# First projection in two half-depth steps between the modulation loads, and the first gates after the second chunk

## The chip, the cores and the metric

The kernel runs on one core of a Trainium2 chip. The time is the device time of one execution in microseconds; of several executions the median counts. Five queues work side by side: TensorE (PE), VectorE (DVE), ScalarE (ACT), GpSimd (POOL) and SyncE (SP), which here issues most of the loads.

## The reference

One layer of a diffusion backbone on 128 context tokens and 256 sample tokens (T = 384 columns), with 1024 channels. What matters for this case is its beginning:

```python
mod = silu(cond) @ w_ada + b_ada            # w_ada: 1024 x 6144
sh1, sc1, g1, sh2, sc2, g2 = split(mod, 6)
h = rmsnorm(x, g_norm1) * (1 + sc1) + sh1
u = h @ w_in                                # w_in: 1024 x 7168
b_c, c_c, v_c, x_r, g_r, m_a, m_b = split(u)
y_a = (b_c * conv3(c_c * v_c)) @ w_conv_out
x_c = conv4(x_r) + rnn_conv_b
# two linear scans over x_c, with gates sigmoid(x_c @ w_gate + b): 8 heads of 128
# then y_b, the merged branches @ w_o, and a mixture of 32 experts of width 512
```

sh1 and sc1 are the first 2048 columns of the modulation: four chunks of 512 columns.

## The kernel before

**Chunks and tiles.** Weights come in chunks of 1024 x 512 (2,048 KB) into a ring of four slots; `chunks` is the order of the loads. SyncE issues chunk n as soon as the one four places before it has been used (L546 to L566). Each chunk gives four output tiles of 128 channels x 384 tokens, m = 0 to 3. `stream` is the order of all tiles, and tile n lies in PSUM bank n % 8, so that a tile can only begin when the tile eight places before it has been read (`open_tile`, `bank_free`). `START` and `W_IN` are the two lists of the work at the beginning: ("par", j) transposes parameters, ("xT", k) transposes a slice of 128 channels of the normalised x, ("adaR", j) multiplies the conditioning with modulation chunk j into rows, ("adaC", j) turns these rows into columns; then come the chunks of `w_in`: ("xr", half), ("c", half), ("v", half) and so on, and a bare number b stands for the gates of two heads, batch b.

**Split products.** The projections multiply in a faster 32-bit form, with both operands split into a high and a low part. A tile takes three products for each slice k of the depth: high weights by low x and by high x (the high parts, L889 and L890; L869 and L870 in the first projection), and low weights by high x (L893; L874). The weights are split by quarters of a chunk, q: ScalarE writes the high part (`feed`, L1262), GpSimd subtracts it for the low part (`write_lo`, L478). There are three pairs of buffers (SUBS = 3). VectorE scales and shifts x (L1699), ScalarE takes its high part (L1316), VectorE its low part (L1692); `h_ready` counts the slices done.

**The first projection** (`first_project`) takes three tiles of ("xr", 0) together, slice by slice, over the whole depth of eight slices, when all four modulation chunks are in; VectorE itself writes the low parts of these three quarters. The fourth tile follows in the usual way. Ahead of it stand products of constants, without use (`constants`, L911).

**Behind the first chunk.** ScalarE copies tile ("xr", h) into one of two padded buffers (`copy_xr`, L1327 and L1328) and, behind the copy, splits the quarter that is three further on (`feed_behind`). From the third copy on it waits for the convolution two tiles before it (`xc_ready`). VectorE convolves (`conv_rnn`: one instruction at L1712, three at L1716), and computes the decay rates once (L1728 to L1742). TensorE's gates for a head (L903) need that head's convolution; ScalarE's sigmoids read them (L1340), and its exponents (L1356, L1361) and a root (L1366) follow, with VectorE between (`gate_inputs`) and behind (`scans`, from L1761). `conv_grid` reads the tiles of ("v", half) from L1792 on. The order on each engine is the order in which the code is written.

Of the kernel before, what the change touches and what calls it, by code (L numbers as in the profile page):

```python
# [40 lines left out]
def layer_program(nc, x_prompt, x_sample, state_rnn, c, c_ctx, w_ada, b_ada, g_norm1, g_norm2, w_in,  # L41
# [71 lines left out]
    def add_gates(b):  # L113
        for h in (2 * b, 2 * b + 1):
            for d in range(2):
# [11 lines left out]
    START = [("par", 0), ("par", 1), ("adaR", 0), ("xT", 0), ("xT", 1), ("xT", 2), ("xT", 3), ("adaR", 1),  # L127
             ("adaC", 0), ("xT", 4), ("xT", 5), ("xT", 6), ("xT", 7), ("adaR", 2), ("adaC", 1),
             ("adaC", 2), ("adaR", 3), ("adaC", 3)]
    stream += START  # L130
    chunks += [("ada", j) for j in range(4)]
    ADA_AFTER = {("v", 0): 4, ("b", 0): 5, ("g", 0): 6, ("c", 1): 7, ("v", 1): 8, ("b", 1): 9, ("g", 1): 10,
                 ("ma", 0): 11}
    for item in W_IN:
        if isinstance(item, int):
            add_gates(item)
        else:
            add_chunk(*item)
# [24 lines left out]
    with ExitStack() as ctx:  # L163
# [160 lines left out]
        first_lo = sem("first_lo_by_vector")  # L324
# [130 lines left out]

        def wait_sub_free(eng, q):

            if q >= SUBS:
                wait_quarter_used(eng, q - SUBS)
# [6 lines left out]
        def wait_split(eng, q):  # L466

            if q < SUBS:
                eng.wait_ge(first_lo, q + 1)
            else:  # L470
                eng.wait_ge(lo_p, q - SUBS + 1)

        def write_lo(eng, q, done):

            src, pair = quarter(q)
            eng.wait_ge(hi_ready, q + 1)
            for ks in (slice(0, KD // 2), slice(KD // 2, KD)):
                last = eng.tensor_tensor(pair[:, 1, ks], src[:, ks], pair[:, 0, ks].bitcast(F32), ALU.subtract)  # L478
            last.then_inc(done, 1)
# [4 lines left out]
        def wait_chunk_used(eng, n):  # L484
# [3 lines left out]
            elif n < NSPLIT:  # L488
                if SPLIT.index(n) == 0:
                    wait_split(eng, SUBS - 1)  # L490
# [169 lines left out]
        def _(eng):  # L660
# [30 lines left out]
            for q in range(SUBS, NQ):  # L691
                write_lo(eng, q, lo_p)
# [103 lines left out]
        def _(eng):  # L796
# [63 lines left out]
            def first_project(kind, x):  # L860

                tiles = [open_tile((kind, m)) for m in range(SUBS)]
                pairs = [quarter(quarter_of(kind, m))[1] for m in range(SUBS)]
                for k in range(KD):
                    eng.wait_ge(h_ready, k + 1)
                    for m in range(SUBS):
                        if k == 0:
                            eng.wait_ge(hi_ready, m + 1)
                        eng.matmul(tiles[m][:, 0:T], pairs[m][:, 0, k, :], x[:, 1, k, :], start=(k == 0), stop=False)  # L869
                        eng.matmul(tiles[m][:, 0:T], pairs[m][:, 0, k, :], x[:, 0, k, :], start=False, stop=False)  # L870
                for m in range(SUBS):
                    wait_split(eng, m)
                    for k in range(KD):
                        mm = eng.matmul(tiles[m][:, 0:T], pairs[m][:, 1, k, :], x[:, 0, k, :],  # L874
                                        start=False, stop=(k == KD - 1))
                    mm.then_inc(tile_done, 1)
                project(kind, 0, x, range(SUBS, CT))

            def project(kind, half, x, ms=range(CT), ready=None):

                for m in ms:
# [3 lines left out]
                    eng.wait_ge(hi_ready, q + 1)  # L885
# [27 lines left out]
            spare = N_OF[("adaR", 2)] % BANKS  # L913
            assert spare == N_OF[("xr", SUBS)] % BANKS
            for name, number in START:
                if (name, number) == ("adaC", 3):
                    constants(spare, 1)
                start_work[name](number)
                if (name, number) == ("adaC", 2):
                    constants(spare, 1)  # L920
            constants(spare, 4)
            for n, item in enumerate(W_IN):
# [4 lines left out]
                else:  # L927
                    if n == 0:
                        first_project(item[0], h_hl)
# [308 lines left out]
        def _(eng):  # L1238
# [13 lines left out]
            fed = [0]  # L1252
# [48 lines left out]
            eng.wait_ge(mean_ready, 1)  # L1301
            eng.activation(stat[:, 0, 2, :], stat[:, 0, 1, :], ACT.Sqrt).then_inc(rms_ready, 1)
# [5 lines left out]
            for name, number in START[2:]:  # L1308
                if name == "xT":
                    ps, free = tile(("xT", number))  # L1310
                    eng.activation(xTr[:, number, :], ps[:, 0:T], ACT.Copy).then_inc(free, 1)
                elif name == "adaR":
                    ada_copy(number)
            for k in range(KD):
                eng.wait_ge(h_whole, k + 1)
                eng.activation(h_hl[:, 0, k, :], xTr[:, k, :], ACT.Copy).then_inc(act_hi, 1)  # L1316
                if 1 <= k <= SUBS:
                    feed(k - 1)
# [49 lines left out]
            def copy_c(half):  # L1368
                for m in range(CT):
# [244 lines left out]
        def _(eng):  # L1614
# [27 lines left out]

            eng.wait_ge(ssq_ready, TT)
# [3 lines left out]
            for t in range(TT):  # L1647
                eng.tensor_scalar(xs[:, t, :], x_in_rows[:, t, :], stat[:, 0, 0, t:t + 1], None, ALU.mult)\
                    .then_inc(xs_ready, 1)
                if t == 1:  # L1650
                    copy_params()
# [29 lines left out]
            for j in range(4):  # L1681
                ada_columns(j)
            for j in range(4):
                wait_read(eng, ("adaC", j))
            for cnd in range(2):
                last = eng.scalar_tensor_tensor(out=A1[:, :, cnd], in0=mod[:, KD:2 * KD, cnd], scalar=1.0,
                                                in1=pT[:, GN1:GN1 + KD], op0=ALU.add, op1=ALU.mult)
# [585 lines left out]
```

## Time and profile before

| | us |
|---|---|
| median of three executions | 949.86 |
| lowest, highest | 949.2, 952.07 |
| the profiled execution | 951.76 |
| its span | 949.7 |

| engine | busy share of the span |
|---|---|
| TensorE | 93% |
| VectorE | 60% |
| GpSimd | 35% |
| ScalarE | 30% |

The busy shares are means over a projection stage of some 390 us, a short stage of routing, and 32 experts. A busy TensorE counts from the start of a matmul to its modelled end, so that two matmuls which follow each other overlap; the distance from start to start is what a matmul costs in a row. The granted clock is given as a share of 2.4 GHz; 0.5 is 1.2 GHz. Times on the left of the rows are microseconds from the start of the span.

### The profile page before, as it was taken

What the parts mean: (1) busy time and instruction counts of PE and PEld (TensorE: products, weight loads), DVE (VectorE), ACT (ScalarE), POOL (GpSimd) and SP (SyncE); (2) the same over time, 40 slices, a digit from 0 to 9 for tenths busy, and PEclk for the clock granted to TensorE, in tenths of its full rate; (3) what the DMA queues carried; (4) which work ended last, traced back from release to release, by engine and by line L of the source; (5) the groups of instructions that cost most, each with busy time, mean ns of one, the idle gap of its engine ahead of it and who ended that gap; (6) DMA issues with size and microseconds to landing.
All of it is one profiled execution on the core that took longest, in us unless ns stands there. A gap on an engine that the chain in (4) does not pass through costs nothing.

```text
span 949.7 us, 12700 instructions
## 1 busy us (share of the span) xinstructions
PE 885.1 (93%) x4502; PEld 551.9 (58%) x4502; DVE 571.0 (60%) x990; ACT 282.9 (30%) x499; POOL 333.4 (35%) x301
## 2 busy tenths in 40 slices
PE   3899999999999999999999999998988988989895
PEld 1579988989999999755444344333333333433331
DVE  2489984677102342236477777775766666766677
ACT  4366374645334332021321121121212121211112
POOL 0046946556556646122222232231313131313100
PEclk9999999999999999999999999999999999999998
DMA  9962556464572537637699999999999999999992
GB/s 344 356 256 89 184 178 220 162 240 172 183 263 91 187 120 250 240 158 291 240 393 411 410 411 419 414 416 402 409 394 415 396 403 389 406 404 408 402 419 87
DMA packets 61882, 285.70 MB, mean 301 GB/s; under 512 B 6895, under 2 KB 11279, under 8 KB 47492
## 3 DMA queue, kind: packets, MB, share of 16 engines
q1 hardware_dynamic: 58228, 278.63, 75.9%
q0 software_dynamic: 2480, 3.11, 1.1%
q10 hardware_dynamic: 1120, 3.24, 0.9%
q8 instruction: 34, 0.56, 0.2%
q14 instruction: 20, 0.16, 0.0%
HBM read 286.80 MB, written 3.19 MB: 305 GB/s over the span
## 4 chain that ended last, share of the span: by engine, by line
PE 65%; DMA 26%; DVE 3%; SPq 2%; ACT 2%; issue 1%; DVEq 0%; ACTq 0%; POOL 0%
DMA ring<-in_w 13%; DMA slot<-in_w 11%; PE bank L889 10%; PE bank L890 10%; PE bank L893 10%; PE bank L1113 9%; PE bank L1130 7%; PE bank L959 4%; PE bank L1114 3%; DMA ring<-in_w_ada 2%; PE bank L1090 2%; PE bank L825 2%; PE bank L903 2%; PE bank L1068 1%; SPq L637 1%
## 5 line engine op out<-in xcount | busy, mean ns | idle before, releaser
L478 POOL TENSOR_TENSOR subs<-ring,subs 128x512 fp32r<-128x512 f32 x138 | 205.5, 1514 | 176.5 <-ACT subs L1262 176.5
L889 PE MATMUL bank<-h_hl,subs 128*128 128x384 f32 x488 | 165.9, 340 | 0.6 <-ACT lru L1340 0.6
L890 PE MATMUL bank<-h_hl,subs 128*128 128x384 f32 x488 | 164.1, 336 | 0.0
L1113 PE MATMUL bank<-ring,x_T 128*64 128x512 f32 x256 | 116.7, 597 | 11.7 <-DMA slot<-in_w 4.3
L1114 PE MATMUL bank<-ring,x_T 128*64 128x512 f32 x256 | 117.1, 598 | 0.0
L2079 DVE TENSOR_TENSOR hg<-hg,lru 128x512 f32<-128x512 f32 x186 | 116.7, 680 | 0.0
L676 POOL COPY idx<-lists 64x1 uint32 (+1 forms) x31 | 5.5, 179 | 297.3 <-PE bank L1068 292.8
L1113 PE MATMUL bank<-slot,x_T 128*64 128x512 f32 x192 | 89.2, 606 | 11.5 <-DMA slot<-in_w 8.2
L1262 ACT ACTIVATE subs<-ring 128x1024 fp32r<-128x1024 f32 x72 | 76.1, 1060 | 72.6 <-PE bank L893 72.6
L889 PEld LDWEIGHTS bank<-h_hl,subs 128*128 128x128 f32 x488 | 91.7, 188 | 5.8 <-issue 4.2
L893 PE MATMUL bank<-h_hl,subs 128*128 128x384 f32 x488 | 94.7, 336 | 0.0
L1554 ACT ACTIVATE lru<-bank 64x512 f32<-64x512 f32 x32 | 19.0, 595 | 247.8 <-PE bank L1114 247.8
L890 PEld LDWEIGHTS bank<-h_hl,subs 128*128 128x128 f32 x488 | 91.7, 188 | 0.4
L1114 PE MATMUL bank<-slot,x_T 128*64 128x512 f32 x192 | 89.6, 607 | 0.0
L893 PEld LDWEIGHTS bank<-h_hl,subs 128*128 128x128 f32 x488 | 85.6, 188 | 0.0
L2070 DVE TENSOR_TENSOR lru<-bank,gain_sample 128x512 f32<-128x512 f32 x124 | 78.9, 674 | 0.0
L2097 DVE SCALAR_TENSOR_TENSOR xcy<-bank,weight_col,lru 64x256 f32<-64x256 f32 x64 | 37.3, 662 | 65.0 <-ACT lru L1554 64.6
L1113 PEld LDWEIGHTS bank<-ring,x_T 128*64 128x64 f32 x256 | 32.7, 136 | 72.5 <-issue 67.2
L2070 DVE TENSOR_TENSOR lru<-bank,cp 128x512 f32<-128x512 f32 x62 | 40.0, 686 | 57.8 <-PE bank L1090 57.8
L689 POOL COPY weight_col<-slot_weight 64x1 f32 (+1 forms) x32 | 69.9, 2187 | 3.2 <-DVE slot_weight L2126 3.2
L1547 ACT ACTIVATE y_hl<-bank 64x512 fp32r<-64x512 f32 x62 | 36.7, 592 | 103.8 <-PE bank L1132 103.1
L1090 PE MATMUL bank<-y_hl,token_oh 128*128 128x512 f32 x186 | 59.4, 427 | 0.0
(249 smaller groups left out, 1504.2 us busy)
## 6 DMA issues: line engine op xcount, KB each, us to landing
ring<-in_w SPq DMA_DIRECT2D x40, 2048.0 KB, 29.2
slot<-in_w SPq DMA_DIRECT2D x30, 2048.0 KB, 29.0
ring<-in_w_in SPq DMA_DIRECT2D x14, 2048.0 KB, 8.0
ring<-in_w_ada SPq DMA_DIRECT2D x12, 2048.0 KB, 8.9
gate_w<-in_w SPq DMA_DIRECT2D x10, 2048.0 KB, 30.0
ring<-in_w SPq DMA_DIRECT2D x16, 1024.0 KB, 31.0
slot<-in_w SPq DMA_DIRECT2D x12, 1024.0 KB, 31.7
ring<-in_w_rnn_out SPq DMA_DIRECT2D x2, 2048.0 KB, 8.3
```

Of the source, the lines that this page charges most:

```text
L478: last = eng.tensor_tensor(pair[:, 1, ks], src[:, ks], pair[:, 0, ks].bitcast(F32), ALU.subtract)
L689: eng.tensor_copy(weight_col[:, s:s + 1], slot_weight[:, bass.ds(e, 1)]).then_inc(weight_cols, 1)
L889: eng.matmul(ps[:, 0:T], pair[:, 0, k, :], x[:, 1, k, :], start=(k == 0), stop=False)
L890: eng.matmul(ps[:, 0:T], pair[:, 0, k, :], x[:, 0, k, :], start=False, stop=False)
L893: mm = eng.matmul(ps[:, 0:T], pair[:, 1, k, :], x[:, 0, k, :], start=False, stop=(k == KD - 1))
L1090: eng.matmul(bank[SPREAD[b % 3]][:, :], token_oh[s % 2][:, t * P:(t + 1) * P], y_hl[:, half, :], start=True, stop=True).then_inc(spread_do ...
L1113: eng.matmul(ps[HALF:P, :], x_T[:, k, :], w1_k[:, k, :], start=(k == 0), stop=(k == KD - 1))
L1114: mm = eng.matmul(ps[0:HALF, :], x_T[:, k, :], w3_k[:, k, :], start=(k == 0), stop=(k == KD - 1))
L1130: eng.matmul(ps[0:HALF, :], zT_buf[:, j * HALF:(j + 1) * HALF], w[:, j, 0:CW], start=(j == 0), stop=(j == JF - 1))
L1262: eng.activation(pair[:, 0], src, ACT.Copy).then_inc(hi_ready, 1)
L2070: eng.tensor_tensor(y_gated[:, b % 3, :], bank[SPREAD[b % 3]][:, :], G2[0 if t == 0 else 1][:, half * CW:(half + 1) * CW], ALU.mult).then_ ...
L2079: eng.tensor_tensor(rows, rows, y_gated[:, b % 3, :], ALU.add).then_inc(added, 1)
```

## The change

The order of the loads becomes modulation 0, modulation 2, ("xr", 0), modulation 1, modulation 3, ("xr", 1): modulation chunks 0 and 2 hold shift and scale of the first four slices of x, chunks 1 and 3 those of the last four. The first projection takes all four tiles of ("xr", 0), first over slices 0 to 3, then over slices 4 to 7, with the products of modulation chunks 1 and 3 between the matmuls of the first half. The weights of ("xr", 0) are split in eight half-quarters r; the last two reuse the buffer of the first two, and `half_used` tells that those are free. GpSimd writes all low parts, and waits for `h_ready` of 4 before the first. VectorE does the scale, the shift and the split of x in two halves. Gates 0 come behind ("xr", 1) instead of ahead of it, on TensorE, ScalarE and VectorE. Silu goes ahead of the root, VectorE's copies of the parameters go first, and of the constants two are left.

```diff
-    W_IN = [("xr", 0), 0, ("xr", 1), ("c", 0), ("v", 0), 1, ("b", 0), ("g", 0), 2, ("c", 1), ("v", 1), 3,
+    W_IN = [("xr", 0), ("xr", 1), 0, ("c", 0), ("v", 0), 1, ("b", 0), ("g", 0), 2, ("c", 1), ("v", 1), 3,
...
+    START = [("par", 0), ("par", 1), ("adaR", 0)] + [("xT", k) for k in range(KD)] + \
+        [("adaR", 2), ("adaC", 0), ("adaC", 2)]
+    stream += START + [("adaR", 1), ("adaC", 1), ("adaR", 3), ("adaC", 3)]
+    chunks += [("ada", 0), ("ada", 2), ("xr", 0), ("ada", 1), ("ada", 3)]
...
+        def half_quarter(r):
+
+            m, k0 = r % CT, (KD // 2) * (r // CT)
+            part = r % (2 * SUBS)
+            cols = slice((part % 2) * (QUART // 2), (part % 2 + 1) * (QUART // 2))
+            return slot_k(C_OF[("xr", 0)])[:, k0:k0 + KD // 2, m * P:(m + 1) * P], \
+                subs[:, part // 2, :, cols].rearrange("p x (k n) -> p x k n", k=KD // 2)
+
         def wait_sub_free(eng, q):
 
-            if q >= SUBS:
+            if q == CT:
+                eng.wait_ge(half_used, 1)
+            else:
                 wait_quarter_used(eng, q - SUBS)
...
-            for q in range(SUBS, NQ):
-                write_lo(eng, q, lo_p)
+            eng.wait_ge(h_ready, CT)
+            for r in range(2 * CT):
+                write_half_lo(eng, r)
+            for q in range(CT, NQ):
+                write_lo(eng, q)
...
+            def first_project(x):
+
+                K2 = KD // 2
+
+                def high_parts(k):
+
                     eng.wait_ge(h_ready, k + 1)
-                    for m in range(SUBS):
+                    for m in range(CT):
+                        r = CT * (k // K2) + m
                         if k == 0:
...
+                        if k % K2 == 0:
+                            eng.wait_ge(hi_ready, r + 1)
+                        ps, pair = bank[N_OF[("xr", m)] % BANKS], half_quarter(r)[1]
+                        eng.matmul(ps[:, 0:T], pair[:, 0, k % K2, :], x[:, 1, k, :], start=(k == 0), stop=False)
+                        eng.matmul(ps[:, 0:T], pair[:, 0, k % K2, :], x[:, 0, k, :], start=False, stop=False)
+
+                def low_parts(r):
+
+                    ps, pair = bank[N_OF[("xr", r % CT)] % BANKS], half_quarter(r)[1]
+                    eng.wait_ge(lo_p, r + 1)
+                    for j in range(K2):
+                        k = K2 * (r // CT) + j
+                        mm = eng.matmul(ps[:, 0:T], pair[:, 1, j, :], x[:, 0, k, :], start=False, stop=(k == KD - 1))
+                    return mm
+
+                for k in range(K2):
+                    if k == K2 - 1:
+                        ada_rows(1)
+                    high_parts(k)
+                low_parts(0)
+                ada_columns(1)
+                low_parts(1)
+                ada_rows(3)
+                low_parts(2)
+                low_parts(3).then_inc(half_used, 1)
+                ada_columns(3)
+                for k in range(K2, KD):
+                    high_parts(k)
+                for m in range(CT):
+                    low_parts(CT + m).then_inc(tile_done, 1)
...
             for name, number in START:
-                if (name, number) == ("adaC", 3):
-                    constants(spare, 1)
                 start_work[name](number)
-                if (name, number) == ("adaC", 2):
-                    constants(spare, 1)
-            constants(spare, 4)
+                if (name, number) == ("adaR", 0):
+                    constants(spare, 2)
...
+            half_hi(4)
+            ada_copy(1)
+            half_hi(5)
+            ada_copy(3)
+            half_hi(6)
+            half_hi(7)
+            h_hi(4)
+            h_hi(5)
+            feed(CT)
+            h_hi(6)
+            h_hi(7)
...
-            copy_xr(2)
-            copy_xr(3)
+            for h in range(2, KD):
+                copy_xr(h)
             gate_sigmoids(0)
             gate_exps(0)
-            copy_xr(4)
-            copy_xr(5)
+            copy_c(0, range(0, 3))
             gate_roots(0)
-            copy_xr(6)
-            copy_xr(7)
-            copy_c(0)
+            copy_c(0, range(3, CT))
...
+            for half in range(2):
+                ks = range(CT * half, CT * (half + 1))
+                for j in (half, 2 + half):
+                    ada_columns(j)
+                for j in (half, 2 + half):
+                    wait_read(eng, ("adaC", j))
...
-            for q in range(SUBS):
-                write_lo(eng, q, first_lo)
...
             decay_rates()
-            conv_rnn(2)
-            conv_rnn(3)
+            for h in range(2, KD):
+                conv_rnn(h)
             gate_inputs(0)
-            for h in range(4, KD):
-                conv_rnn(h)
             scans(0)
```

TensorE before, from the first modulation rows to the first projection (ring and cvec: modulation rows; ident and lru: transposes of x; selc and xcy: modulation columns; iota and ones: constants):

```order
L825 MATMUL bank<-ring,cvec 32x512 x8
L814 MATMUL bank<-ident,lru 128x128 x12
L825 MATMUL bank<-ring,cvec 32x512 x8
L835 MATMUL bank<-selc,xcy 128x2 x4
L814 MATMUL bank<-ident,lru 128x128 x12
L825 MATMUL bank<-ring,cvec 32x512 x8
L835 MATMUL bank<-selc,xcy 128x2 x8
L911 MATMUL bank<-iota,ones 128x384
L825 MATMUL bank<-ring,cvec 32x512 x8
L911 MATMUL bank<-iota,ones 128x384
L835 MATMUL bank<-selc,xcy 128x2 x4
L911 MATMUL bank<-iota,ones 128x384 x4
```

TensorE now, from the first modulation rows to the end of the first half of the sums (L890 the high parts, of which the repeats are left out, L899 the low parts):

```order
L841 MATMUL bank<-ring,cvec 32x512 x8
L950 MATMUL bank<-iota,ones 128x384 x2
L830 MATMUL bank<-ident,lru 128x128 x24
L841 MATMUL bank<-ring,cvec 32x512 x8
L851 MATMUL bank<-selc,xcy 128x2 x8
...
L841 MATMUL bank<-ring,cvec 32x512 x8
...
L899 MATMUL bank<-h_hl,subs 128x384 x4
L851 MATMUL bank<-selc,xcy 128x2 x4
L899 MATMUL bank<-h_hl,subs 128x384 x4
L841 MATMUL bank<-ring,cvec 32x512 x8
L899 MATMUL bank<-h_hl,subs 128x384 x8
L851 MATMUL bank<-selc,xcy 128x2 x4
```

Two of the four modulation products moved behind the first matmuls of the projection; the columns product of chunk 3 is now the last thing ahead of its second half, and the four constants that stood ahead of the projection are gone.

ScalarE before, around the first sigmoids (xrp: copy of an ("xr", h) tile, subs: high part of a quarter, lru<-bank: sigmoids):

```order
L1327 ACTIVATE xrp<-bank 128x128
L1328 ACTIVATE xrp<-bank 128x256
L1262 ACTIVATE subs<-ring 128x1024
L1340 ACT_TABLE_LOAD
L1340 ACTIVATE lru<-bank,pT 128x387 x8
L1356 ACT_TABLE_LOAD
L1356 ACTIVATE lru<-lru,rate 128x387 x4
L1361 ACTIVATE lru<-lru,rate 128x387 x4
L1327 ACTIVATE xrp<-bank 128x128
```

ScalarE now, at the same sigmoids (cp: copy of a ("c", m) tile):

```order
L1393 ACTIVATE xrp<-bank 128x128
L1394 ACTIVATE xrp<-bank 128x256
L1297 ACTIVATE subs<-ring 128x1024
L1406 ACT_TABLE_LOAD
L1406 ACTIVATE lru<-bank,pT 128x387 x8
L1422 ACT_TABLE_LOAD
L1422 ACTIVATE lru<-lru,rate 128x387 x4
L1427 ACTIVATE lru<-lru,rate 128x387 x4
L1439 ACTIVATE cp<-bank 128x128
```

Before, the copies ahead of the sigmoids were those of tiles 0 to 3 and the other four followed; now all eight stand ahead, each with a quarter's high part from the third on, and the tiles of ("c", 0) follow.

## Rows read from the trace of the kernel before

**Rows 1.** The page: busy time, share of the span and instructions of each engine.

```profile
PE 885.1 (93%) x4502; PEld 551.9 (58%) x4502; DVE 571.0 (60%) x990; ACT 282.9 (30%) x499; POOL 333.4 (35%) x301
```

**Rows 2.** Waits of TensorE, 66 to 560 us: total, times, longest.

```profile
PE bank L968 <- DVE hg L1917: 1.2, 1, 1.2
...
```

**Rows 3.** Chain of waits, 0 to 150 us: start, us, what.

```profile
10.47 19.72 DMA ring<-in_w_ada
```

**Rows 4.** Timeline of TensorE: start, us to last end, instructions, idle before and releaser.

```profile
16.02 3.64 PE L825 MATMUL bank<-ring,cvec 128*32 128x512 f32 x16 [6.30 <-ACT cvec L1306]
19.59 1.63 PE L814 MATMUL bank<-ident,lru 128*128 128x128 f32 x12
...
25.36 1.92 PE L825 MATMUL bank<-ring,cvec 128*32 128x512 f32 x16
27.21 1.95 PE L835 MATMUL bank<-selc,xcy 128*128 128x2 f32 x16
29.02 0.89 PE L911 MATMUL bank<-iota,ones 128*128 128x384 f32 x2
30.33 3.47 PE L825 MATMUL bank<-ring,cvec 128*32 128x512 f32 x16 [0.42 <-DMA ring<-in_w_ada]
...
35.49 2.83 PE L911 MATMUL bank<-iota,ones 128*128 128x384 f32 x8
...
49.60 4.32 PE L874 MATMUL bank<-h_hl,subs 128*128 128x384 f32 x24
...
57.93 2.76 PE L903 MATMUL bank<-xcy,gate_w 128*128 128x387 f32 x8
62.20 2.87 PE L903 MATMUL bank<-xcy,gate_w 128*128 128x387 f32 x8 [1.51 <-DVE xcy L1716]
...
82.43 0.34 PE L889 MATMUL bank<-h_hl,subs 128*128 128x384 f32 x1
...
117.66 5.47 PE L903 MATMUL bank<-xcy,gate_w 128*128 128x387 f32 x16
```

**Rows 5.** Stretches: length, busy PE, PEld, DVE, ACT, POOL, granted clock, DMA share, GB/s.

```profile
30.00:32.00 2.00, 1.67 (x8) 0.46 (x12) 0.00 (x0) 0.00 (x0) 0.00 (x0) 0.52 1.05 385
32.00:34.00 2.00, 2.00 (x13) 0.50 (x6) 0.00 (x0) 0.14 (x1) 0.00 (x0) 0.63 1.06 390
...
60.00:62.00 2.00, 0.69 (x3) 0.07 (x1) 1.96 (x2) 0.00 (x0) 1.72 (x2) 1.00 1.05 398
```

**Rows 6.** Timeline of VectorE.

```profile
37.65 0.56 DVE L1692 TENSOR_TENSOR h_hl<-hg,h_hl 128x384 fp32r<-128x384 f32 x1
...
57.53 4.61 DVE L1716 SCALAR_TENSOR_TENSOR xcy<-xrp,pT,xcy 128x387 f32<-128x387 f32 x3
62.06 0.16 DVE L1728 TENSOR_SCALAR sp<-sp 128x16 f32<-128x16 f32 x1
...
67.42 0.48 DVE L1712 TENSOR_SCALAR xcy<-xrp,pT 128x387 f32<-128x387 f32 x1
67.93 1.94 DVE L1716 SCALAR_TENSOR_TENSOR xcy<-xrp,pT,xcy 128x387 f32<-128x387 f32 x3
...
98.94 2.86 DVE L1761 TENSOR_TENSOR lru<-lru 128x1548 f32<-128x1548 f32 x1
...
120.41 0.41 DVE L1793 TENSOR_TENSOR cp<-bank,cp 128x256 f32<-128x256 f32 x1
```

**Rows 7.** Timeline of GpSimd: low parts beside the first convolutions.

```profile
52.83 8.89 POOL L478 TENSOR_TENSOR subs<-ring,subs 128x512 fp32r<-128x512 f32 x6 [50.38 <-ACT subs L1262]
```

**Rows 8.** Timeline of ScalarE: a copy, a quarter's high part, the first sigmoids.

```profile
62.24 0.28 ACT L1327 ACTIVATE xrp<-bank 128x128 f32<-128x128 f32 x1 [4.33 <-DVE xcy L1716]
...
62.67 1.06 ACT L1262 ACTIVATE subs<-ring 128x1024 fp32r<-128x1024 f32 x1
63.75 1.28 ACT L1340 ACT_TABLE_LOAD   x1
65.05 3.91 ACT L1340 ACTIVATE lru<-bank,pT 128x387 f32<-128x387 f32 x8
```

More of the change, by code:

```diff
@@ L137, in layer_program @@
         else:
-            add_chunk(*item)
+            if item == ("xr", 0):
+                stream += [("xr", m) for m in range(CT)]
+            else:
+                add_chunk(*item)
             if item in ADA_AFTER:
@@ L466, in wait_split, with write_lo, write_half_lo @@
         def wait_split(eng, q):
[L468 to L473, printed above, removed]
+            eng.wait_ge(lo_p, q + CT + 1)
+        def write_lo(eng, q):
             src, pair = quarter(q)
-            eng.wait_ge(hi_ready, q + 1)
+            eng.wait_ge(hi_ready, q + CT + 1)
             for ks in (slice(0, KD // 2), slice(KD // 2, KD)):
                 last = eng.tensor_tensor(pair[:, 1, ks], src[:, ks], pair[:, 0, ks].bitcast(F32), ALU.subtract)
-            last.then_inc(done, 1)
+            last.then_inc(lo_p, 1)
+        def write_half_lo(eng, r):
+            src, pair = half_quarter(r)
+            eng.wait_ge(hi_ready, r + 1)
+            eng.tensor_tensor(pair[:, 1], src, pair[:, 0].bitcast(F32), ALU.subtract).then_inc(lo_p, 1)
         def wait_chunk(eng, n):
@@ L867, in first_project @@
                         if k == 0:
[L868 to L876, printed above, removed]
@@ L1250, in tile @@
                 return bank[n % BANKS], bank_free[n % BANKS]
-            fed = [0]
+            fed = [CT]
             def feed(last_q):
@@ L1307, in _, with copy_xT, half_hi, h_hi @@
                            ACT.Silu).then_inc(cvec_ready, 1)
[L1308 to L1314, printed above, removed]
+            eng.wait_ge(mean_ready, 1)
+            eng.activation(stat[:, 0, 2, :], stat[:, 0, 1, :], ACT.Sqrt).then_inc(rms_ready, 1)
+            def copy_xT(k):
+                ps, free = tile(("xT", k))
+                eng.activation(xTr[:, k, :], ps[:, 0:T], ACT.Copy).then_inc(free, 1)
+            def half_hi(r):
+                src, pair = half_quarter(r)
+                if r == 0:
+                    wait_chunk(eng, C_OF[("xr", 0)])
+                if r == 2 * SUBS:
+                    eng.wait_ge(half_used, 1)
+                eng.activation(pair[:, 0], src, ACT.Copy).then_inc(hi_ready, 1)
+            def h_hi(k):
                 eng.wait_ge(h_whole, k + 1)
                 eng.activation(h_hl[:, 0, k, :], xTr[:, k, :], ACT.Copy).then_inc(act_hi, 1)
-                if 1 <= k <= SUBS:
-                    feed(k - 1)
+            ada_copy(0)
+            for k in range(KD):
+                copy_xT(k)
+            ada_copy(2)
+            half_hi(0)
+            half_hi(1)
+            h_hi(0)
+            half_hi(2)
+            h_hi(1)
+            half_hi(3)
+            h_hi(2)
+            h_hi(3)
+            half_hi(4)
[9 more added lines that the diff above has]
+            h_hi(7)
             eng.wait_ge(pads_zero, 2)
@@ L1366, in gate_roots, with copy_c @@
                 eng.activation(r_f, r_f, ACT.Sqrt).then_inc(root_done, 1)
-            def copy_c(half):
-                for m in range(CT):
+            def copy_c(half, ms=range(CT)):
+                for m in ms:
                     ps, free = tile(("c", CT * half + m))
@@ L1679, in norm2_gain @@
                         .then_inc(gain_ready, 1)
[L1681 to L1687, printed above, removed]
-            then(last)
             def split_lo(x_hl, x, k, count, done):
```

55 lines of the change are left out of this document (24 added, 31 removed).

## The prediction

> **What bounds the kernel now.** I read the page first: TensorE is busy for 93% of the span [rows 1]. Its waits come next: between 66 and 560 us it waits four times, none of them longer than 1.2 us [rows 2]. So whatever makes the projections start earlier or later reaches the experts almost unchanged, and the experts' loads, which fill the transfer engines later, are issued as TensorE sets slots free, so they move along. The case is decided before that. There the chain of waits stands on the modulation loads until 30.19 us (10.47 + 19.72) [rows 3]; then come the last modulation rows, and the first projection, which ends at 57.93 [rows 4]. Behind it TensorE waits 1.51 us for the convolution before the second half of gates 0, and the tiles of ("c", 0) begin at 82.43 [rows 4]. VectorE's convolutions, beside GpSimd, are the second thing to read [rows 6, 7]. My measure is the moment C at which ("c", 0) begins; up to there the change permutes and splits work, and behind it the order is the old one.
>
> **The loads.** 385 GB/s [rows 5] give 5.4 us for a chunk of 2,048 KB. Counted back from 30.19, the chunks land near 13.9, 19.4, 24.8 and 30.2, and counted on at 35.6 and 41.0. In the new order these are modulation 0, 2, then ("xr", 0), modulation 1, 3, then ("xr", 1). SyncE now holds ("c", 0) and all loads queued behind it until the eight half-splits are done; by the sum below that is about 47 us, and the chunk is first split beyond 70, so this wait is free.
>
> **Up to the first half of the sums.** Silu is moved ahead of the root and the parameter copies to the front of VectorE; Silu, which released TensorE at 16.02 [rows 4], then ends before the first chunk lands, and the chunk sets the start: 13.9. The rows of x fall back by one table load (1.28) [rows 8] and are still there before the transposes. On TensorE, counted from start to start: modulation rows 0 take 3.57 (nothing has warmed TensorE up, as now), two constants 1.4 (four take 2.83), 24 transposes 3.1 (12 take 1.56), rows 2 1.85, columns 0 and 2 1.81 [rows 4]: 13.9 + 11.8 = 25.7. From the end of the last columns (35.49) to the end of the first low half of x (37.65 + 0.56) pass 2.7 us [rows 4, 6]; so the first matmul stands at 28.4.
>
> The first half holds 32 high and 16 low matmuls at 0.173 each (48 from 49.60 to 57.93) [rows 4], 8.3 us, and modulation rows 1 and 3 (2 x 1.85) and columns 1 and 3 (1.8) stand between: 13.8. Neither chunk is late: TensorE comes to rows 1 past 32 and to rows 3 past 37 us. So the half ends at 42.2, or 43.7 if it begins at the low clock.
>
> **The clock.** At 30.33 TensorE had waited only 0.42 us, yet rows 3 took 3.47 instead of 1.92, with a granted clock of 0.52 and 0.63 (partly at 1.2 GHz, partly at 2.4); ahead of them stood the thin columns products [rows 4, 5]. After the wait of 1.51 at 60.7 the clock stayed at 1.00 [rows 4, 5]. The change takes away four of six constants, and puts thin columns and then 2.7 to 3.9 us of waiting ahead of each half. I take the lower clock at both: 3.47 - 1.92 = 1.55 us each; the bounds are 0 and 3.64 - 1.92 = 1.7. The Trainium skill, "TensorE: Matmul & The Clock Gate", section "HAM oscillation — how this bites in real kernels", speaks against the change: bursts of matmuls with waits between them start at the low clock each time. By that rule the third wait below costs its whole 1.55 too, and the sum would be 953.4; by the row at 60.7 alone no wait costs anything, and it would be about 949 (the trace here has both cases).
>
> **The second half.** Columns 3 end at 43.7. The same 2.7 us of VectorE and ScalarE follow, but now not alone: GpSimd, held until four slices of x are split, has done six of the eight low halves, and the last two only become possible when the first sums are used, which is exactly then. Beside GpSimd, VectorE's instructions take 1.5 instead of 0.5 to 0.65 [rows 6, 7]; two so hit add 1.2 (bounds 0, and 3 with later slices hit as well). Start at 47.6; 32 + 16 matmuls 8.3, and the clock 1.55: the four tiles end at T = 57.5. Today three of them end at 53.9 and the fourth at 57.93 [rows 4]. So the early start earns 0.4 us here: it is spent in the wait for columns 3. With no low clock and no contention T is 53.2.
>
> **Gates a chunk later.** TensorE's own work from T is four tiles (16.6, 24 x 0.173 each) and the gates (5.5) [rows 4]: C = T + 22.1. This removes the wait of 1.51. What is late next: the gates' tiles reuse the banks of ("xr", ...), and ScalarE now copies all eight before it takes the first sigmoid. Each copy from the third on waits for the convolution two before it (two buffers). So C follows VectorE:
> - copy of tile 0 done at T - 1.4 (twelve low matmuls before T, then 0.6 for the copy [rows 8]);
> - six convolutions, each 2.4 alone and 6.1 beside GpSimd (three steps in 4.61, the fourth likewise) [rows 6]. GpSimd has idle time here, for it is fed behind each copy; I lay its pairs of instructions (2 x 1.48) [rows 7] beside them: 2.4, 3.1, 2.4, 3.2, 5.1, 3.3 = 19.5 (bounds 14.4 and 24);
> - the decay rates between the second and third: 62.06 to 67.42, 5.4 [rows 6];
> - last copy 0.55, the quarter's high part behind it 1.0, table load 1.28, first sigmoid 0.5 [rows 8]: 3.4.
>
> Sum: -1.4 + 19.5 + 5.4 + 3.4 = 26.9. C = 57.5 + 26.9 = 84.4, where TensorE could have begun at 79.6; on the way it also waits about 1 us for the fourth quarter of ("xr", 1), which costs nothing, as the banks come later. So +2.0 against 82.43. TensorE then has nearly nothing to do for 4 us; between no loss (as at 60.7) and 1.55 I take 0.8. **Sum: +2.8 us.**
>
> Other edits: SyncE's issues, the splitting of the high parts into halves and the first lows, moved from VectorE to GpSimd, lie inside these waits. Behind C, scans 0 begin today 16.5 us after C (98.94) [rows 6]; in the new order ScalarE's exponents, three copies and the root give about C + 17, beside a GpSimd as full as today, and the bank of the last ("v", 0) tile, free at 120.82, is needed by the seventh tile of gates 1 at 117.66 + 6 x 0.68 = 121.8 [rows 4, 6]: still 1 us of room, less 0.5.
>
> The profiled execution took 951.76 for a span of 949.7; with +2.8 it would be 954.6. The median is 949.86, 1.9 lower, so the forecast for the median is 949.86 + 2.8 = **952.7 us**.
>
> **Rivals.**
> 1. *The early half pays (faster).* The clock stays up and GpSimd misses the x split: T = 53.2; the convolutions run nearly alone (5 us less): C = 53.2 + 22.1 to 24.5, some 5 us before 82.43. Time 945. For it: at 60.7 a wait did not lower the clock, and GpSimd has little to do after T. Against: the row at 30.33, and the 1.5 us steps as soon as GpSimd runs. Partial forms (T = 55, C = T + 25) give -2.4.
> 2. *The scans come too late (slower).* If the exponents and the root of gates 0 slip by 3 us more against C (convolutions 6 and 7 fully beside GpSimd, 6.1 each), the last bank of ("v", 0) is late for the seventh tile of gates 1 and adds 2.5 to the sum: +5.3, 955. It decides as soon as that bank is free later than C + 39. For it: the room is 1 us. Against: the chain behind C is as long as the old one.
> 3. *It only swaps waits.* TensorE loses and gains the same, C within 1 us of 82.43: 950, inside the spread of my own case.
>
> **Chances.** About 0.3% (2.85 us) is what can be told from no change here. My own case, with rival 3, spreads over -2 to +5: T moves by 1.5 with the clock, the chain of convolutions by 2. It has 0.62, rival 1 with its partial forms 0.25, rival 2 0.13. Faster: nearly all of rival 1, 0.24. Slower: rival 2 and 0.27 of my own, 0.40. Same: 0.36. My own case alone reaches from 948 to 955; with rival 1's price below and rival 2's above, 944.5 to 956.5.
>
> **What would show it.** Right: the first high matmul near 28; a wait of 3 us or more after columns 3; the four tiles ended near 57; all eight copies of ("xr", ...) ahead of the sigmoids, and TensorE waiting for a sigmoid just before ("c", 0), at about 84; granted clock under 1.00 near 28, 47 or 84. Wrong: the tiles ended by 54; ("c", 0) released by TensorE's own work and not by ScalarE; no low clock; or gates 1 waiting for VectorE's product with ("v", 0).

## The result, and the profile after

The changed kernel took 957.60 us (median of 5, from 955.95 to 958.75), the kernel before 949.86 beside it (median of 5, from 948.34 to 952.07). The ratio is 1.0085, with an interval from 1.007 to 1.010: slower by 7.7 us, where 2.8 were forecast. The direction was right; the time lies outside the range.

The page shows a small difference: the sum of TensorE's busy time grew by 3.6 us [rows 1], and the granted clock sank in the second to fourth slice.

```profile
PE 888.7 (93%) x4494; PEld 557.5 (58%) x4494; DVE 562.4 (59%) x986; ACT 283.1 (30%) x503; POOL 330.1 (35%) x307
...
PEclk9888999999999999999999999999999999999998
```

TensorE's waits (total, times, longest), from 0 to 66 us and, behind the gap, from 66 to 570:

```profile
PE bank L890 <- DVE h_hl L1746: 6.7, 2, 4.1
...
PE bank L928 <- ACT subs L1297: 2.7, 1, 2.7
PE bank L928 <- ACT lru L1406: 1.9, 1, 1.9
PE bank L1003 <- DVE hg L1979: 1.2, 1, 1.2
...
PE bank L942 <- ACT xrp L1394: 0.5, 1, 0.5
```

The 1.2 us were there before [rows 2]. The waits of 2.7, 1.9 and 0.5 us behind 66 are new, and all three name ScalarE. TensorE's timeline (start, us to the last end, instructions, idle before and releaser; L890 and L891 are the high parts in `first_project`, L899 the low parts, L928 the high parts of a later tile, L841 modulation rows, L851 columns, L942 gates) shows where each stands:

```profile
27.80 0.69 PE L890 MATMUL bank<-h_hl,subs 128*128 128x384 f32 x1 [2.59 <-DVE h_hl L1746]
28.29 0.52 PE L891 MATMUL bank<-h_hl,subs 128*128 128x384 f32 x1
28.61 0.52 PE L890 MATMUL bank<-h_hl,subs 128*128 128x384 f32 x1
...
34.05 0.34 PE L891 MATMUL bank<-h_hl,subs 128*128 128x384 f32 x1
34.22 0.34 PE L890 MATMUL bank<-h_hl,subs 128*128 128x384 f32 x1
...
35.02 1.92 PE L841 MATMUL bank<-ring,cvec 128*32 128x512 f32 x16
...
44.09 0.95 PE L851 MATMUL bank<-selc,xcy 128*128 128x2 f32 x8
49.16 0.69 PE L890 MATMUL bank<-h_hl,subs 128*128 128x384 f32 x1 [4.12 <-DVE h_hl L1746]
...
60.04 0.34 PE L928 MATMUL bank<-h_hl,subs 128*128 128x384 f32 x1
...
75.37 0.66 PE L928 MATMUL bank<-h_hl,subs 128*128 128x384 f32 x1 [2.69 <-ACT subs L1297]
...
86.19 0.92 PE L942 MATMUL bank<-xcy,gate_w 128*128 128x387 f32 x2 [0.47 <-ACT xrp L1394]
89.03 0.69 PE L928 MATMUL bank<-h_hl,subs 128*128 128x384 f32 x1 [1.92 <-ACT lru L1406]
...
123.89 1.92 PE L841 MATMUL bank<-ring,cvec 128*32 128x512 f32 x16
```

At 28.3 one matmul follows the other after 0.32 us, at 34.1 after 0.173: the same instruction at the lower and at the full clock. The four tiles end at T = 60.04 instead of 57.93 [rows 4] and C is 89.03 instead of 82.43, so 4.5 of the 6.6 us lost up to C lie between T and C. I add one mark, the start of modulation rows 4, 33 to 35 us behind C: 123.89 here, 115.80 in the trace of before, 8.1 us.

The span of the profiled execution grew by only 6.0, since the trace of before shows 2.1 us elsewhere which this one lacks: at the router's constants the clock is 0.67 and 0.50 (340 to 344 us) there, and 1.00 here. Of the ten profiles told of here five have that drop and five not, with no part of the change in common; its cause stays open, and single spans are compared only up to the mark.

Stretches of 2 us (busy PE, PEld, DVE, ACT, POOL; granted clock, DMA share, GB/s), where rows 5 had 0.52 and 0.63 in two of them:

```profile
28.00:30.00 2.00, 2.00 (x7) 2.00 (x8) 1.84 (x6) 1.55 (x5) 0.00 (x0) 0.50 1.05 386
...
48.00:50.00 2.00, 0.83 (x3) 0.84 (x4) 1.92 (x6) 1.94 (x4) 0.00 (x0) 0.50 0.58 123
50.00:52.00 2.00, 2.00 (x8) 2.00 (x7) 2.00 (x3) 0.39 (x1) 1.95 (x2) 0.50 1.05 408
...
54.00:56.00 2.00, 2.00 (x12) 2.00 (x11) 0.36 (x1) 0.00 (x0) 0.00 (x0) 0.87 1.06 391
...
90.00:92.00 2.00, 2.00 (x8) 2.00 (x7) 1.93 (x4) 2.00 (x5) 0.17 (x1) 0.50 0.00 0
```

In each half seven or eight matmuls fit into 2 us at 0.50, where thirteen fit at 1.00 in the row of e3 below (2 us by 0.173 would be eleven to twelve, and those that overlap the edges count too). Counted from its first matmul, the first half stays at the low clock for 6.2 us (27.80 to 34.0) and the second for 5.4 (49.16 to 54.5). The low clock comes back behind C. It also stands behind the wait of 2.69 us (0.50 from 76 to 78 us); there it doesn't move C, which follows VectorE's chain, as the rows below and e8 show.

VectorE, first at the second half of x (L1765 scale and shift, L1746 low part), then at the convolutions (L1776, L1780) and the decay rates (L1792 to L1806):

```profile
46.40 2.08 DVE L1765 TENSOR_SCALAR hg<-hg,A,mod 128x128 f32<-128x128 f32 x4
48.55 0.56 DVE L1746 TENSOR_TENSOR h_hl<-hg,h_hl 128x384 fp32r<-128x384 f32 x1
...
58.80 0.48 DVE L1776 TENSOR_SCALAR xcy<-xrp,pT 128x387 f32<-128x387 f32 x1 [4.45 <-ACT xrp L1394]
...
64.57 1.26 DVE L1792 TENSOR_SCALAR sp<-sp 128x16 f32<-128x16 f32 x1
...
66.15 0.17 DVE L1794 TENSOR_TENSOR sp<-sp 128x16 f32<-128x16 f32 x1
66.36 1.28 DVE L1795 TENSOR_TENSOR sp<-sp 128x16 f32<-128x16 f32 x1
67.68 1.22 DVE L1796 TENSOR_SCALAR sp<-sp 128x16 f32<-128x16 f32 x1
68.93 1.43 DVE L1798 SCALAR_TENSOR_TENSOR sp<-sp 128x16 f32<-128x16 f32 x7
...
71.18 0.48 DVE L1776 TENSOR_SCALAR xcy<-xrp,pT 128x387 f32<-128x387 f32 x1
```

GpSimd at the same two places (L494 half-quarters, L487 whole quarters):

```profile
45.00 2.48 POOL L494 TENSOR_TENSOR subs<-ring,subs 128x512 fp32r<-128x512 f32 x2 [5.51 <-ACT subs L1355]
...
62.94 2.86 POOL L487 TENSOR_TENSOR subs<-ring,subs 128x512 fp32r<-128x512 f32 x2 [10.38 <-ACT subs L1297]
66.32 2.54 POOL L487 TENSOR_TENSOR subs<-ring,subs 128x512 fp32r<-128x512 f32 x2 [0.52 <-ACT subs L1297]
```

From 45.00 to 47.48 GpSimd writes the last two half-quarters, beside VectorE's steps. From 62.94 to 68.86 its two pairs stand beside the end of a convolution and the decay rates: three of the rates' instructions, on only 16 columns, take 1.2 to 1.3 us, where one of the same size between the pairs takes 0.17.

In the trace of before one pair already stood beside the rates, and hit the seven steps that take 1.43 here (VectorE, GpSimd):

```profile
63.18 3.41 DVE L1734 SCALAR_TENSOR_TENSOR sp<-sp 128x16 f32<-128x16 f32 x7
...
63.81 2.54 POOL L478 TENSOR_TENSOR subs<-ring,subs 128x512 fp32r<-128x512 f32 x2 [2.09 <-ACT subs L1262]
```

So the rates took 5.4 us there with one pair beside them [rows 6], and 71.18 - 64.57 = 6.6 here with the two.

ScalarE at the end of the chain (L1393 the last copy of ("xr", 1), L1406 the sigmoids):

```profile
85.59 0.28 ACT L1393 ACTIVATE xrp<-bank 128x128 f32<-128x128 f32 x1 [1.86 <-DVE xcy L1780]
...
87.10 1.28 ACT L1406 ACT_TABLE_LOAD   x1
88.40 3.90 ACT L1406 ACTIVATE lru<-bank,pT 128x387 f32<-128x387 f32 x8
```

The last copy waits for VectorE's sixth convolution, and C follows it by 89.03 - 85.59 = 3.4 us.

### The profile page after: what moved, and what is told of

It reads as the page before. It is cut to its first block, busy times and chain, and to the rows that moved or that the text cites. A ratio compares the mean times of both kernels' runs of the same rounds, so it can differ in the third digit from the quotient of the medians.

```text
span 955.7 us, 12693 instructions
## 1 busy us (share of the span) xinstructions
PE 888.7 (93%) x4494; PEld 557.5 (58%) x4494; DVE 562.4 (59%) x986; ACT 283.1 (30%) x503; POOL 330.1 (35%) x307
## 4 chain that ended last, share of the span: by engine, by line
PE 66%; DMA 25%; DVE 5%; SPq 2%; ACT 1%; issue 1%; DVEq 0%; ACTq 0%; POOL 0%
DMA ring<-in_w 17%; PE bank L1148 10%; PE bank L928 10%; PE bank L929 9%; PE bank L932 9%; PE bank L1165 7%; PE bank L994 4%; DMA slot<-in_w 4%; DMA gate_w<-in_w 4%; PE bank L1149 3%; PE bank L841 2%; PE bank L1125 2%; PE bank L942 2%; DVE xcy L1780 2%; PE bank L1103 1%
## 5 line engine op out<-in xcount | busy, mean ns | idle before, releaser
L487 POOL TENSOR_TENSOR subs<-ring,subs 128x512 fp32r<-128x512 f32 x136 | 199.5, 1490 | 144.0 <-ACT subs L1297 144.0
L928 PE MATMUL bank<-h_hl,subs 128*128 128x384 f32 x480 | 165.2, 344 | 4.6 <-ACT subs L1297 2.7
L1148 PE MATMUL bank<-ring,x_T 128*64 128x512 f32 x256 | 118.4, 604 | 13.0 <-DMA ring<-in_w 5.9
L1149 PE MATMUL bank<-ring,x_T 128*64 128x512 f32 x256 | 120.5, 613 | 0.0
L928 PEld LDWEIGHTS bank<-h_hl,subs 128*128 128x128 f32 x480 | 91.6, 191 | 10.1 <-issue 7.2
L1148 PE MATMUL bank<-slot,x_T 128*64 128x512 f32 x192 | 87.6, 597 | 8.5 <-DMA slot<-in_w 4.6
L1297 ACT ACTIVATE subs<-ring 128x1024 fp32r<-128x1024 f32 x68 | 71.8, 1059 | 71.0 <-PE bank L932 71.0
L1149 PE MATMUL bank<-slot,x_T 128*64 128x512 f32 x192 | 87.9, 598 | 0.0
L1148 PEld LDWEIGHTS bank<-ring,x_T 128*64 128x64 f32 x256 | 32.9, 137 | 74.4 <-issue 69.5
L702 POOL COPY weight_col<-slot_weight 64x1 f32 (+1 forms) x32 | 63.4, 1982 | 3.2 <-DVE slot_weight L2188 3.2
L1125 PE MATMUL bank<-y_hl,token_oh 128*128 128x512 f32 x186 | 59.4, 427 | 0.0
## 6 DMA issues: line engine op xcount, KB each, us to landing
gate_w<-in_w SPq DMA_DIRECT2D x10, 2048.0 KB, 29.4
```

The costliest lines, as they stand in the source:

```text
L702: eng.tensor_copy(weight_col[:, s:s + 1], slot_weight[:, bass.ds(e, 1)]).then_inc(weight_cols, 1)
L928: eng.matmul(ps[:, 0:T], pair[:, 0, k, :], x[:, 1, k, :], start=(k == 0), stop=False)
L1125: eng.matmul(bank[SPREAD[b % 3]][:, :], token_oh[s % 2][:, t * P:(t + 1) * P], y_hl[:, half, :], start=True, stop=True).then_inc(spread_do ...
L1148: eng.matmul(ps[HALF:P, :], x_T[:, k, :], w1_k[:, k, :], start=(k == 0), stop=(k == KD - 1))
L1149: mm = eng.matmul(ps[0:HALF, :], x_T[:, k, :], w3_k[:, k, :], start=(k == 0), stop=(k == KD - 1))
L1297: eng.activation(pair[:, 0], src, ACT.Copy).then_inc(hi_ready, 1)
```

## The experiments

The theory: the loss has two parts. (a) Gates 0 a chunk later put all of VectorE's chain ahead of C. (b) The two halves of the first projection run at the low clock, and GpSimd makes the wait between them longer. Rivals: the early half by itself is the loss; the low clock costs nothing at the end; the third wait at C, not VectorE's chain, holds ("c", 0) up. The median of before was 949.24 in the session of the first four kernels and 949.44 in that of the other four. In the table, differences are against these, and those of the mark against 115.80. T, C and the mark are read from the one profiled execution, the median from all; the ratio that stands with each run has a 95% interval. For e2 and e4 the ratio is some 1.5 us above the difference of the medians.

| kernel | T | C | mark, difference | median | difference |
|---|---|---|---|---|---|
| changed kernel | 60.0 | 89.0 | +8.1 | 957.60 | +7.7 |
| e1_gates_back | 59.5 | 84.4 | +2.1 | 951.80 | +2.6 |
| e2_warm | 56.0 | 85.0 | +4.3 | 955.75 | +6.5 |
| e3_hold | 55.1 | 84.9 | +4.8 | 954.93 | +5.7 |
| e4_before_gates_later | 58.0 | 85.5 | +5.2 | 955.20 | +6.0 |
| e5_back_warm_hold | 53.4 | 79.0 | -2.8 | 947.38 | -2.1 |
| e6_back_hold | 58.3 | 83.2 | +0.9 | 949.49 | 0.0 |
| e7_before_no_constants | 59.2 | 83.7 | +1.2 | 950.92 | +1.5 |
| e8_decay_later | 59.4 | 84.6 | +3.6 | 953.66 | +4.2 |

(In the kernel before, T is 57.9 and C 82.4. In e1, e5, e6 and e7, as there, gates 0 stand between T and ("xr", 1); the work between T and C is the same in all rows. Where a wait follows T, T is 0.17 behind the start of the last matmul.)

**e1_gates_back: the changed kernel with gates 0 in their old place on TensorE, ScalarE and VectorE.**

```diff
-    W_IN = [("xr", 0), ("xr", 1), 0, ("c", 0), ...
+    W_IN = [("xr", 0), 0, ("xr", 1), ("c", 0), ...
...
-            for h in range(2, KD):
-                copy_xr(h)
+            copy_xr(2)
+            copy_xr(3)
             gate_sigmoids(0)
             gate_exps(0)
-            copy_c(0, range(0, 3))
+            copy_xr(4)
+            copy_xr(5)
             gate_roots(0)
-            copy_c(0, range(3, CT))
+            copy_xr(6)
+            copy_xr(7)
+            copy_c(0)
```

(VectorE's order goes back in the same way.)

> The changed kernel with gates 0 put back between the two chunks on TensorE, ScalarE and VectorE; the rest of the change stays. Theory (the late gates cost a wait for all eight copies, about 4.3 us, and 1.5 us of low clock behind it): the first projection still ends near 60 us, (c, 0) begins near 84.7 instead of 89.0, the time falls by 5 to 6 us, to about 952. Rival (the late gates only swap one wait for another, the loss is all in the first projection): (c, 0) within 1 us of 89, time within 1.5 us of 957.6.

Measured: 951.80, ratio 1.0024 [1.0010, 1.0038]. The later gates cost 7.7 - 2.6 = 5.1 us, as the theory said, and ("c", 0) begins at 84.35, where 84.7 was expected. What is left, 2.6, comes with the rest of the change; e5 and e6 below tie it to the halves. Up to T this kernel issues what the changed one does, so it shows how much the low clock varies: the first 24 matmuls took 34.90 - 28.94 = 5.96 us here and 35.02 - 27.80 = 7.22 in the changed kernel's profile, against 24 x 0.173 = 4.15.

**e2_warm: constants ahead of each half.**

```diff
+                open_tile(("xr", 0))
+                constants(N_OF[("xr", 0)] % BANKS, 4)
                 for k in range(K2):
...
                 ada_columns(3)
+                constants(N_OF[("adaR", 1)] % BANKS, 5)
                 for k in range(K2, KD):
```

> The changed kernel with constants products in TensorE's two waits: four ahead of the first half of the first projection, five ahead of the second. Theory (the low clock lengthens both halves, 6 us each at half speed): the granted clock stays at 1.00, the first half is 2.9 us shorter, the slices of x come 2.9 us earlier, and the projection ends near 55.5 instead of 60.0, as the last slice then sets it; time 953 (952 to 954.5). Rival (the waits for x set the end and the clock is hidden in them): the projection ends within 1 us of 60, time within 1.5 us of 957.6.

Measured: 955.75, ratio 1.0084 [1.0067, 1.0101]. The clock is 1.00 from 28 to 58 us, T falls by 4.0 and the mark by 3.8: in the profiled execution the low clock in the halves lay on the path to the mark. The whole time doesn't show it. The profiled execution (953.76, 3.8 below that of the changed kernel, and like it without the drop at the router's constants) is the lowest of four; the median is 955.75 where 953 was expected, 1.9 below the changed kernel's; and by the ratio nothing is gained (1.0084 against 1.0085). Why stays open; e5 and e6 below, with twelve executions each, show a gain of the whole time. The clock at C is still low (0.80, 0.50, 0.85 from 84 to 90 us).

**e3_hold: GpSimd writes the seventh half-quarter only when all of x is split.**

```diff
             for r in range(2 * CT):
+                if r == 2 * SUBS:
+                    eng.wait_ge(h_ready, KD)
                 write_half_lo(eng, r)
```

> The changed kernel with GpSimd also held, before its seventh half-quarter, until all eight slices of x are split. Theory (GpSimd beside VectorE delays the fifth slice by some 1.5 us and the eighth by 3): the fifth slice is ready near 47.6 instead of 49.1, the second half, still at the low clock, ends 1.5 us earlier, time about 956. Rival (the contention is hidden, or the later low parts now come late): no change, 957.6, or slower by 1 to 2 us with TensorE waiting for the low parts.

Measured: 954.93, ratio 1.0064 [1.0047, 1.0081]. The wait between the halves and what follows, on VectorE:

```profile
44.71 1.25 DVE L1767 TENSOR_SCALAR hg<-hg,A,mod 128x128 f32<-128x128 f32 x4
46.04 0.56 DVE L1748 TENSOR_TENSOR h_hl<-hg,h_hl 128x384 fp32r<-128x384 f32 x1
...
53.85 1.35 DVE L1778 TENSOR_SCALAR xcy<-xrp,pT 128x387 f32<-128x387 f32 x1 [3.98 <-ACT xrp L1396]
```

on TensorE:

```profile
46.65 0.44 PE L892 MATMUL bank<-h_hl,subs 128*128 128x384 f32 x1 [2.59 <-DVE h_hl L1748]
...
71.28 0.41 PE L930 MATMUL bank<-h_hl,subs 128*128 128x384 f32 x1 [3.55 <-ACT subs L1299]
```

and in a stretch of the second half:

```profile
48.00:50.00 2.00, 2.00 (x13) 2.00 (x12) 1.25 (x3) 0.53 (x1) 0.05 (x1) 1.00 0.02 4
```

Without GpSimd the four steps take 1.25 instead of 2.08, and the one ahead of them (the gain of x) 0.24 instead of 0.94; the wait is 2.59 instead of 4.12: the contention was 1.5. In this execution the second half then keeps its clock, which is more than expected, and the time is 1 us below the expected 956. T falls by 5.0, but C only by 4.1: GpSimd's later pairs now meet the first convolution, whose first step takes 1.35 instead of 0.48, and the fourth quarter of ("xr", 1) comes from the same VectorE chain, so that TensorE waits 3.55 instead of 2.69 for it.

**e4_before_gates_later: the kernel before, with the gates alone a chunk later.** The edit is that of e1, the other way round, on the kernel before.

> The kernel before with this one edit of the change: gates 0 behind the second chunk on TensorE, ScalarE and VectorE. Theory: the first projection ends at 57.9 as before, all six convolutions come ahead of the last copy, (c, 0) begins near 85.2 instead of 82.4 and starts at the low clock, time 953 to 954.5. Rival (a mere swap, or a gain of the 1.5 us wait removed): 948.5 to 950.5.

Measured: 955.20, ratio 1.0078 [1.0062, 1.0095]. TensorE:

```profile
82.67 0.92 PE L903 MATMUL bank<-xcy,gate_w 128*128 128x387 f32 x2 [1.78 <-ACT xrp L1328]
85.52 0.69 PE L889 MATMUL bank<-h_hl,subs 128*128 128x384 f32 x1 [1.93 <-ACT lru L1340]
```

T moves by 0.1, and C is 85.52, 3.1 later. The mark is 2.1 later still: 1.5 by the low clock behind C, the rest because a tile's 24 matmuls take 4.24 us in this execution from 90 us on, against 4.16 in before. So this part alone slows the kernel before by 6.0 us (7.4 by the ratio), above the expected 953 to 954.5, with the old first projection. That the early half is the whole loss is refuted.

**e8_decay_later: the changed kernel with the decay rates behind the sixth convolution.**

```diff
+            for h in range(2, 6):
+                conv_rnn(h)
             decay_rates()
-            for h in range(2, KD):
+            for h in range(6, KD):
                 conv_rnn(h)
```

> The changed kernel with VectorE's decay rates behind the sixth convolution instead of the second, nothing else. Theory (the six convolutions and the decay rates in one chain set the last copy, the sigmoids and so the start of (c, 0)): the last copy comes 6 us earlier, TensorE waits little, (c, 0) begins near 83.3 instead of 89.0, at a higher clock; time 951 to 952.5. Rival (ScalarE's copies and quarters or TensorE's own work set it): (c, 0) near 88, time 956 to 957.6.

Measured: 953.66, ratio 1.0042 [1.0026, 1.0058], 1.2 us above the expected range. On VectorE:

```profile
58.13 0.48 DVE L1776 TENSOR_SCALAR xcy<-xrp,pT 128x387 f32<-128x387 f32 x1 [4.01 <-ACT xrp L1394]
...
80.94 1.23 DVE L1792 TENSOR_SCALAR sp<-sp 128x16 f32<-128x16 f32 x1
```

and TensorE:

```profile
84.56 0.69 PE L928 MATMUL bank<-h_hl,subs 128*128 128x384 f32 x1 [1.92 <-ACT lru L1406]
```

The six convolutions now take 80.94 - 58.13 = 22.8 us, against 26.8 with the decay rates among them, and C falls by 4.5, of which 0.7 is an earlier T. Of the 6.6 us taken out, 2.6 come back: without the rates the convolutions meet more of GpSimd's pairs. The wait for the first sigmoid is 1.92 in both, so it isn't the wait that holds ("c", 0) up but the chain ahead of it: C follows VectorE, and not TensorE's own work.

**e5_back_warm_hold: e1, e2 (four constants at each place) and e3 together.**

> The changed kernel with all three edits of the runs before: gates 0 back between the two chunks, constants in the two waits (four and four), GpSimd held for its last two half-quarters until x is split. Theory (the three losses add up and the half-depth order itself pays): the first projection ends near 53.2 us at a granted clock of 1.00, (c, 0) begins near 77.5, 5 us earlier than in the kernel before; time 944 (943 to 946) where the kernel before takes 949.5. Rival (the earlier projection is eaten by VectorE's scans, whose banks the second gates need): no faster than the kernel before, TensorE waiting for VectorE near 112 us.

Measured: 947.38, ratio 0.9973 [0.9963, 0.9983]: faster than both kernels, but by 2.1 us and not by 5. TensorE:

```profile
50.59 2.99 PE L901 MATMUL bank<-h_hl,subs 128*128 128x384 f32 x16
55.46 2.84 PE L947 MATMUL bank<-xcy,gate_w 128*128 128x387 f32 x8 [1.88 <-issue]
...
62.25 0.44 PE L933 MATMUL bank<-h_hl,subs 128*128 128x384 f32 x1 [0.61 <-ACT lru L1411]
```

and VectorE's first convolution:

```profile
52.15 1.24 DVE L1784 TENSOR_SCALAR xcy<-xrp,pT 128x387 f32<-128x387 f32 x1 [4.09 <-ACT xrp L1399]
53.42 1.93 DVE L1788 SCALAR_TENSOR_TENSOR xcy<-xrp,pT,xcy 128x387 f32<-128x387 f32 x3
```

The clock is 1.00 from 28 to 58 us and T is 53.4, 4.5 earlier than before. The view calls the wait of 1.88 "issue", but the gates start 0.1 us after the first convolution ends at 55.35: it is that convolution they waited for, which before lay beside the fourth tile. Its first step took 1.24 beside GpSimd's held pairs; in e6, where it took 0.48, the same wait is 1.16. ("xr", 1) begins at 62.25 and ("c", 0) at 79.00, both 3.4 earlier than in before (77.5 was expected for the second); the rest of T's 4.5 goes into this wait. At the mark 2.8 are left, since the tiles behind C take 4.24 us instead of 4.16 in this execution, as in e4.

**e6_back_hold: e5 without the constants.**

> The run before without the constants: gates 0 back and GpSimd held. Theory: the first half runs at the low clock for 3.4 to 6 us, the second perhaps; the projection ends near 55, (c, 0) begins near 79.5; time 946 to 947.5, 2 to 3 us above the run with constants. Rival (with the shorter wait the clock needs no constants): within 1 us of the run with constants.

Measured: 949.49, ratio 0.9999 [0.9986, 1.0013]. The clock is low again in both halves (0.50 from 30 to 32 and from 48 to 52 us), T is 58.3 and C 83.2: later than the 55 and 79.5 expected, and the time is 2 us above the expected range. The constants are worth 2.1 us of the median (the intervals of e5 and e6 don't touch), so the rival that the low clock costs nothing at the end falls. At the mark they are worth 3.7; the profile of e5 has the drop at the router's constants and that of e6 hasn't. With gates 0 in their old place the early half thus stands at +2.6 us (e1), 0.0 with GpSimd held, and -2.1 with the constants too. The second half begins behind the same wait of 2.59 as in e3, there at the full clock, here at the low one: the wait alone doesn't decide.

**e7_before_no_constants: the kernel before without its six constants.**

```diff
             for name, number in START:
-                if (name, number) == ("adaC", 3):
-                    constants(spare, 1)
                 start_work[name](number)
-                if (name, number) == ("adaC", 2):
-                    constants(spare, 1)
-            constants(spare, 4)
```

> The kernel before without its six constants products. Theory (they keep the clock up over the thin columns and the waits for x): the first projection starts at 39 to 42 us at the low clock, ends 1.7 to 3 us later than 57.9, and the time rises by as much, to 951 to 952.5. Rival (the clock does not depend on them): no change, or 0.2 to 0.9 us less, as columns 3 come a little earlier.

Measured: 950.92, ratio 1.0010 [0.9999, 1.0022]: the interval touches no change, the sign is as expected and the size smaller. The first projection begins at the low clock:

```profile
40.00:42.00 2.00, 1.57 (x4) 1.06 (x5) 1.72 (x6) 2.00 (x5) 0.00 (x0) 0.50 1.18 299
```

The four tiles end 1.2 us later, where 1.7 to 3 were expected; C and the mark move by the same 1.2.

## Why the prediction was right in sign and wrong in size

The steps in their order, read from the profile of the changed kernel (us):

| step | forecast | measured | off by |
|---|---|---|---|
| first matmul | 28.4 | 27.80 | -0.6 |
| low clock in the first half | 1.55 | 7.22 - 4.15 = 3.1 | +1.5 |
| the rest of the first half | 13.8 | 4.15 + 10.02 = 14.2 | +0.4 |
| the wait ahead of the second | 3.9 | 4.12 | +0.2 |
| second half with its low clock | 9.85 | 10.88 | +1.0 |
| T | 57.5 | 60.04 | +2.5 |
| copy of tile 0 against T | -1.4 | -1.2 | +0.2 |
| six convolutions | 19.5 | 20.2 | +0.7 |
| decay rates | 5.4 | 6.6 | +1.2 |
| from the last copy to C | 3.4 | 3.4 | 0 |
| C | 84.4 | 89.03 | +4.6 |
| low clock behind C | 0.8 | 1.5 | +0.7 |
| sum | +2.8 | +8.1 | +5.3 |

**The step that failed most** is "The clock": "I take the lower clock at both: 3.47 - 1.92 = 1.55 us each; the bounds are 0 and 3.64 - 1.92 = 1.7". It measured 3.1 and 10.88 - 8.3 = 2.6 (1.8 and 2.1 in e1), above the bound. I took the extra time of one row (3.47 - 1.92) [rows 4] as the price of a low clock, though it was only the price of the stay in that place, 3.2 us (30.3 to 33.5; ahead of it stood a constant product as well as the thin columns [rows 4]). In the halves the stay was 6.2 and 5.4, and each us at 0.50 costs half a us. e2 shows that T follows this price (4.0 us), and e5 against e6 that it reaches the whole time (2.1 us). With it "the early start earns 0.4 us here" turned into a loss: T is 2.1 later than before, and the early half alone costs 2.6 us (e1). The sign of the sum came right by the other part, the later gates.

The rule of the Trainium skill, "TensorE: Matmul & The Clock Gate", section "HAM oscillation — how this bites in real kernels", which I set against the change, was the better guide: both halves and ("c", 0) began at the low clock. It differed from my forecast only at the third wait, to which it gives the whole price: 1.5 was measured there, against my 0.8. With it the sum would have been 953.4, still too low, since the price of one start was too small and the decay rates were, too. Behind a wait of 2.59 us both outcomes occur here: the second half begins at 1.00 in e3 and at 0.50 in e6.

**The second step** is "the decay rates between the second and third: 62.06 to 67.42, 5.4". It measured 6.6. I carried over a duration with the neighbour that it had then: one of GpSimd's pairs stood beside the rates before, and two stand there now, those of the quarters fed behind the copies 2 and 3. The convolutions, for which I did lay these pairs, were off by only 0.7.

**What held.** The mechanism of C: all eight copies ahead of the sigmoids, ScalarE releasing ("c", 0), and VectorE's chain behind it (e4, e8). The contention ahead of the second half: two of VectorE's steps were hit, as laid out, and it was 1.5 for the forecast 1.2 (e3). SyncE's late issue of ("c", 0) cost nothing: no wait of TensorE behind T names a load before the experts.

**The rivals.** The first (the early half pays) came near only when both of its conditions were built in and the gates stayed where they were: e5, T = 53.4 against its 53.2, and 2.1 us gained instead of 5. That the half-depth order earns these 2.1, and not the earlier Silu that came with it, was not tested by itself. The second (scans too late) had the nearest time, but not by its mechanism: no wait for VectorE's product with ("v", 0) appears, and TensorE's waits behind C are those of before. The third (waits are only swapped) needed C within 1 us of 82.43 and fell with 89.03; e4 shows that the swap alone costs 3.1 us of C.

## What to carry to other kernels

Two reorderings in one change are priced one by one: here a useful one (the new first projection, with constants and a GpSimd that waits: -2.1 us in e5) stood beside one that put a whole VectorE chain ahead of TensorE (+5 to +6). Before moving a consumer behind one more chunk, follow the slowest producer's chain up to the new place, with every small instruction that lies in it, and ask which of them GpSimd will newly stand beside, and how often. Price a burst behind a wait by its own stay at the low clock, with room above, not by one row of other work.

## What was not expected of the hardware

- VectorE's instructions on 128 x 16 elements took 1.22 to 1.28 us beside GpSimd, instead of 0.17, and a step of a convolution (128 x 387) took 1.4 to 1.5 there, instead of 0.5 to 0.65. So about 1 us was added at either size, and a chain of small instructions loses most in proportion.
- The same instructions behind the same waits met different clocks: 3.5 us at the low clock in e1 (29.4 to 32.9) and 6.2 in the changed kernel (27.8 to 34.0) in the first half; 1.00 in e3 and 0.50 in e6 in the second.
- At a granted clock of 1.00 a tile's 24 matmuls took 4.16 us in some stretches and 4.24 in others (between 94 and 111 us: 4.16 in the kernel before and in the changed one, 4.24 in e3, e4 and e5). The cause stays open.
